# Attention in a two-layer decoder trunk: value products and divisions one query block behind the transposed probabilities

## The reference

```python
def causal_attention(q, k, v):
    ...
    def one_block(args):
        blk, qi = args
        sc = jnp.einsum("bqhd,bkhd->bhqk", qi, k).astype(jnp.float32)
        q_idx = blk * Q_BLOCK + jnp.arange(Q_BLOCK)
        sc = jnp.where(key_idx[None, :] <= q_idx[:, None], sc, neg)
        p = jax.nn.softmax(sc, axis=-1).astype(v.dtype)
        return jnp.einsum("bhqk,bkhd->bqhd", p, v)
```

## Time and profile before

| | before |
|---|---|
| median of 3 runs | 2352.89 us (2352.69 to 2354.26) |
| the profiled execution, its own time | 2351.72 us |
| its span | 2349.9 us |
| granted TensorE clock, mean over the span | 0.991 |
| busy: PE, DVE, ACT, POOL | 97%, 57%, 38%, 44% |
| attention stage, 205 to 425 us of the span | 220.0 us, PE busy 201.8 |

### The profile page before, as it was taken

One profiled execution on the slowest core, in us unless ns is written; L12 is line 12 of the kernel. 1 busy time (PEld: TensorE's weight loads), 2 busy tenths in 40 slices (PEclk: granted clock), 3 DMA queues, 4 the chain that ended last, 5 costly groups with the idle time before them and its releaser, 6 DMA issues.

```text
span 2349.9 us, 31829 instructions
## 1 busy us (share of the span) xinstructions
PE 2276.1 (97%) x10415; PEld 1850.8 (79%) x10415; DVE 1337.8 (57%) x2177; ACT 903.8 (38%) x1595; POOL 1034.3 (44%) x715
## 2 busy tenths in 40 slices
PE   6998999999999999999989999999999999999998
PEld 5786777778888888888868878878788888888886
DVE  7756565248755555555671115663875555555556
ACT  4535555124433333333441114451433333333333
POOL 3413333333555555555433332214335555555554
PEclk9999999999999999999999999999999999999998
DMA  4100000311111111111231110012111111111112
GB/s 167 45 27 1 1 0 28 117 36 45 37 54 53 47 52 46 52 54 54 64 124 55 45 45 28 27 56 92 34 36 54 54 53 47 52 46 52 54 54 90
DMA packets 34583, 122.07 MB, mean 52 GB/s; under 512 B 3840, under 2 KB 3968, under 8 KB 34240
## 3 DMA queue, kind: packets, MB, share of 16 engines
q1 hardware_dynamic: 31328, 105.39, 14.3%
q10 hardware_dynamic: 3168, 15.54, 1.7%
HBM read 112.52 MB, written 8.39 MB: 51 GB/s over the span
## 4 chain that ended last, share of the span: by engine, by line
PE 89%; DVE 7%; ACT 2%; issue 2%; POOL 0%; DMA 0%; ACTq 0%; DVEq 0%; POOLq 0%
PE ps L808 10%; PE ps L806 10%; PE ps L810 10%; PE ps L728 9%; PE ps L730 9%; PE ps L729 9%; PE ps L846 6%; PE ps L848 6%; PE ps L847 6%; PE ps L1571 2%; PE ps L1718 1%; PE ps L1722 1%; PE ps L1720 1%; PE ps L1559 1%; PE ps L603 1%
## 5 line engine op out<-in xcount | busy, mean ns | idle before, releaser
L509 POOL TENSOR_TENSOR wlo<-stage,whi 128x512 fp32r<-128x512 f32 x308 | 397.3, 1295 | 459.4 <-ACT whi L971 455.5
L728 PE MATMUL ps<-ahi,whi 128*128 128x512 f32 x896 | 368.8, 412 | 29.8 <-POOL wlo L434 19.1
L427 POOL TENSOR_TENSOR whi<-stage,cons 128x1024 fp32r<-128x1024 f32 x64 | 125.5, 1962 | 527.8 <-PE ps L730 313.4
L730 PE MATMUL ps<-ahi,wlo 128*128 128x512 f32 x896 | 351.2, 392 | 0.0
L729 PE MATMUL ps<-alo,whi 128*128 128x512 f32 x896 | 351.0, 392 | 0.0
L971 ACT CAST whi<-stage 128x512 fp32r<-128x512 f32 x308 | 189.2, 620 | 363.5 <-POOL stage L522 181.0
L1231 DVE TENSOR_TENSOR hT<-hT,ps 128x512 f32<-128x512 f32 x352 | 238.9, 686 | 153.9 <-PE ps L848 153.8
L846 PE MATMUL ps<-hid_hi,whi 128*128 128x512 f32 x640 | 251.3, 393 | 1.8 <-DVE hT L1231 1.6
L848 PE MATMUL ps<-hid_hi,wlo 128*128 128x512 f32 x640 | 249.8, 390 | 0.0
L847 PE MATMUL ps<-hid_lo,whi 128*128 128x512 f32 x640 | 249.6, 390 | 0.0
L806 PE MATMUL ps<-ahi,whi 128*128 128x512 f32 x608 | 236.7, 389 | 0.0
(11 more groups left out here) (323 smaller groups left out, 4089.6 us busy)
## 6 DMA issues: line engine op xcount, KB each, us to landing
stage<-in_wt SPq DMA_DIRECT2D x184, 512.0 KB, 3.6
hT<-in_xt SPq DMA_DIRECT2D x16, 256.0 KB, 9.6
hT<-in_xt ACTq DMA_DIRECT2D x8, 512.0 KB, 8.3
spill<-hT ACTq DMA_DIRECT2D x1, 4096.0 KB, 12.1
hT<-spill ACTq DMA_DIRECT2D x8, 512.0 KB, 8.2
out<-hT SPq DMA_DIRECT2D x16, 256.0 KB, 2.1
wqb_s<-in_wqb ACTq DMA_DIRECT2D x1, 1024.0 KB, 4.8
wlru_s<-in_wlru ACTq DMA_DIRECT2D x1, 512.0 KB, 6.4
```

What stands on the lines that cost most here:

```text
L509: nc.gpsimd.tensor_tensor(block_lo(c), src, block_hi(c).bitcast(F32), ALU.subtract).then_inc(sem(L + "b_ready"), 1)
L728: nc.tensor.matmul(bank, hi, rhs_k[0][:, tok], start=k_first, stop=False)
L730: return nc.tensor.matmul(bank, lo, rhs_k[0][:, tok], start=False, stop=k_last)
```

## The change

TensorE runs `weigh` for the step before, behind the transposes, scores and projection of the present step; the first step of a pair has none, and the last has two, its own behind that of step 14. VectorE does the same with `outputs`. The turns stay where they were, as do the queues of ScalarE, GpSimd and SyncE.

```diff
@@ TensorE, head_pair
                     if k < 4 and not (last and par == 1):
                         project(p * 2 + par + 1, 1 - par, k)
-                    weigh(p * 2 + par, k, step, grp)
+                    for before in ([i - 1] if i >= 1 else []) + ([i] if i == 15 else []):
+                        was, kb = before // 8, before % 8
+                        weigh(p * 2 + was, kb, p * 16 + before, p * 24 + (12 * was + groups_before[kb]))
                     for n, (slot, _, _) in enumerate(turns):
                         if par == 1 and slot == k:
                             turn(p, n, last)
@@ VectorE, head_pair
                     if k < 2 and not (last and par == 1):
                         rotate(p * 2 + par + 1, k)
-                    outputs(p, par, k, p * 16 + i)
+                    for before in ([i - 1] if i >= 1 else []) + ([i] if i == 15 else []):
+                        outputs(p, before // 8, before % 8, p * 16 + before)
                     for n, (slot, _, _) in enumerate(turns):
                         if par == 1 and k == min(slot + 1, 7):
                             y_lo(p, n)
```

## The result

| | before | with the change |
|---|---|---|
| median | 2352.85 us (2352.29 to 2354.26, 8 runs) | 2359.9 us (2357.89 to 2361.42, 8 runs) |
| ratio of the medians | | 1.0027, 95% interval 1.0018 to 1.0036 |
| profiled execution | 2351.72 us, span 2349.9 | 2359.52 us, span 2357.1 |
| granted TensorE clock, mean | 0.991 | 0.990 |
| second turn of pair 1, 2, 3, 4 starts at | 263.83, 318.14, 372.48, 423.63 | 266.20, 323.36, 379.88, 430.05 |

The changed kernel is slower by 0.27%, some 6.4 us by the ratio. Before: 54.31, 54.34, 51.15 us. With the change: 57.16, 56.52, 50.17.

The account below looks back on a forecast made before the run. TensorE, busy 97% of the span, was taken to bound the kernel. The profiled 2351.7 us plus 4.7 for the engines and 1.1 for the clock made 2357.5, with the median 1.2 higher at 2358.7; range 2350 to 2364.

Parts of the forecast that it names:

- term 1: First head's second projection: the moved value products no longer cover the scaling and rotation chain; cost 1.51 us per pair.
- term 2: Third projection of both heads: seven blocks of value products cover where eight stood; cost 0.22 us each, 0.44 per pair.
- term 3: Second head's second projection: four blocks cover instead of seven, and ScalarE is 0.45 us late; cost 1.02 us per pair.
- term 4: Value products' waits for copies of the transposed probabilities are removed; gain 1.88 us per pair.
- term 5: Step 5's transposes wait for the bank that step 4's first copy empties; cost 0.25 us per pair.
- term 6: Pair's end: step 15's value products wait for step 14's division, queued behind the next pair's maximum; cost 0.73 us per pair.
- term 7: Turn 1's wait and the first projection's 1.3 us wait for the pair's last turn both stay; later GpSimd splits cost nothing.
- last pair at full clock: Last pair: second head has no projections, so the lag has other work to run; the pair gives 1.5 us back.
- clock term: Pair ends: deeper gaps make three clock falls instead of one, 0.55 us each; +1.1 us.
- A: Waits ahead of value products go and nothing replaces them, saving 10.8 us; 2342.1 us, chance 0.08.
- B: About even: second-head and pair-end costs smaller, slow stretch at the stage's end shorter; 2349.8 to 2355.0 us, chance 0.27.
- C: The clock falls at every gap, +5.0 us instead of +1.1; 2362.6 us, chance 0.15.

Follow-up runs that it names:

- e12: The change plus six unread dummy matmuls in each gap, ahead of the first head's second projection and between the flushed value products; 2356.9 us, ratio 1.0013.
- e5: Kernel before, with the lag only in steps 0 to 3 of the first head in the loop's pairs, caught up in step 4; 2359.12 us, ratio 1.0024.
- e8: Kernel before, lag only from step 4 of heads, taken up before scores of steps 7 and 15, those divisions before the maximum; last head lagged throughout; 2346.42 us.
- e11: e8 with the first head's lag begun one step earlier, at step 3; 2346.75 us, ratio 0.997.
- e1: Kernel before, with the lag in the last pair alone; 2351.04 us, ratio 0.9985.
- e2: The change, with the last pair back in the old order, so the lag is in the loop alone; 2361.11 us, ratio 1.0033.
- e4: The change, with step 14's value products ahead of step 15's scores and their division ahead of the maximum, in the loop; 2356.27 us, ratio 1.001.
- e7: Kernel before, with only step 14's value products and division deferred to step 15 in the loop, the flush alone; 2359.45 us, ratio 1.0027.
- e6: The change, with step 0's value products back in step 0 and none in step 1, moving the gap behind the second projection; 2365.92 us, ratio 1.0058.
- e9: The change plus twelve unread dummy matmuls in each gap, ahead of the first head's second projection and between the flushed value products; 2362.21 us, ratio 1.0038.
- e10: e6 plus twelve unread dummy matmuls in each gap, ahead of the first head's third projection and at the pair's end; 2363.5 us, ratio 1.004.

## Why the prediction was right

The median came out 1.2 us above the forecast, and it is the case that was forecast, not another with the same sum. Term by term, with the full-clock pairs of e12:

| step | predicted | measured |
|---|---|---|
| P(0) to P(1), first head (term 1) | 4.46 us, a gap of 1.80 | 4.45, idle 1.61 (records overlap) |
| P(1) to P(2) (term 2) | 0.22 open | idle 0.22 and 0.24 |
| P(0) to P(1), second head (term 3) | 4.46 + 0.45 = 4.91 | 4.86 |
| copy waits (term 4) | all gone | no row left |
| T(5), first head (term 5) | 0.25 | 0.19 |
| end of the pair (term 6) | +0.73 | +0.84 |
| turns (term 7) | unchanged | 3.2 and 2.0, as before |
| loop pair at full clock | +2.07 | +2.2 (56.53 against 54.32) |
| last pair at full clock | -1.5 | -1.4 (48.28 against 49.7) |
| clock | +1.1 | +1.0 in the stage |

The 0.84 of term 6: from the last score's end (319.62, worked out from its start and 0.39 us) to W(15) are 2.12 us and from there to the turn 1.62, 3.74 in all, less W(14) with its 0.61; before, 0.66 and 1.63. The 49.7 is an estimate: e5 has the last pair of before, 50.22 us with one slow stretch, less the 0.55 that the prediction read for one. By the prices found below it may be off by 0.3.

The three loop pairs cost the engines 2.2 us each (the first, from P(0) to its turn, 53.93 against 51.74) and the last pair gives 1.4 back: 5.2 us, predicted 4.7. Another 0.2 stands ahead of the first P(0) (212.27 against 212.09), where nothing was moved. For the clock, the change is 2.5 us over e12 behind the first turn (0.6 in the second pair, 1.9 in the last), and before has 1.5 in its last pair (51.15 against the estimate of 49.7): 1.0 more, predicted 1.1. The three make the 6.4 us between 423.63 and 430.05. The slow stretch at the start of the stage is no part of this: it lasts to 212 both in before and in the change. In e12 it ends at 209, ahead of the first dummy, and its P(0) comes 0.8 us earlier for a reason that is not the filling.

Another 0.8 of the span's 7.2 lies behind the stage, where nothing was to move. One row of PE's waits there differs, first of before, then of the change:

```profile
PE ps L620 <- DVE diag L681: 4.5, 3, 2.2
```

```profile
PE ps L620 <- DVE diag L681: 6.3, 3, 3.8
```

The same row has 6.3 us in e8 and e12, and 4.4 and 4.3 in e5 and e11. It follows no part of the change; I take it for scatter between executions, which no run was made to show. In the traces of this case the part of the span behind the last turn took between 1925.0 us (e11) and 1931.2 (e1), with the same code.

In the last pair the new waits were as listed (W(7) 0.36 and W(11) 0.54 for 0.55 each, T(13) 0.32 for 0.3, W(15) 0.45 for 0.5), but for T(9) with 0.31, which was not foreseen, and W(14), which did not wait.

The signs that the prediction had named came too: PE's idle time ahead of the first projection matmul is 10.4 us (9.7 and 0.7), no product waits for a copy, W(15) waits 1.50 us, the loop pairs take over 56 and the last is shorter. Its limit of three slow stretches is met only if the one at the start of the stage, which it did not count in before either, is left out.

**What was off is the make-up of the clock term.** Its total came out by luck, since three things came otherwise than counted and offset each other. The count was too high: three falls at the loop's pair ends were forecast and two came. The price, "a fall costs 0.55, as the waits swallow the rest", holds for the short stretches: those of some 3.4 us cost 0.4 and 0.7 in two pairs of e2, 0.65 in e4 and in e5, 0.8 in e1 and 0.6 in the change. It fails for the one at the third pair's end, which lasted from 379.3 to 386.2, twice as long, and cost 1.9; P(1) came 5.70 us behind P(0) there (382.82 to 388.52), so no wait took it up. And the fall of before at 420.1, ahead of its last turn and worth 0.9 of the 1.5, was kept in the sum; in the change it came at 430.5, behind the last turn. So, with the estimate of 49.7, +0.6, +1.3 and -0.9 stand where two times 0.55 was forecast. In e7 and e6 no such offset helped, and the excess was 1.0 to 1.3 and 2.5 to 4.7 us a pair.

**The rivals.** A was wrong where it said it would be, at P(1) 4.45 us behind P(0); e1 shows the piece of it that is true, in the last pair. B needed terms 3 and 6 to be smaller; they were 0.97 (4.86 less 4.46, and the 0.57 of cover) and 0.84, for 1.02 and 0.73. C, the clock at every gap, didn't come for the change, whose second pair end stayed at 1.00; e6, with the gap one interval on, is nearly that case.

The Trainium skill, page TensorE: Matmul & The Clock Gate, section Loop structure matters more than you think, has matmuls stay at full clock when they run back to back, and lose it at a long wait for a DMA between them. e12 agrees with the first, at 1.00 until 427 with its gaps filled. The prediction carried the second over to short waits, of which the section says nothing: here the clock fell in a kernel with gaps of at most 1.61 us, and stayed up with them filled; the change's second pair end, with a gap of 1.50 us and a clock of 1.00, shows that not every one does.

**What stays open**: why the clock fell at some of the equal gaps and not at others, also between executions of the same code, so that the count of slow stretches in one trace is only a rough one; and why the gap ahead of P(2) brought more slow stretches than the one ahead of P(1). And e8 is 8.2 us ahead at the last turn (415.46 against 423.63) but 6.2 at the end of the span; the row on diag holds 1.8 of that.

## What to carry to other kernels

Before work is moved out of the way of a wait, ask what chain it covers where it stands: 1.5 us of value products under a projection's scaling and rotation were worth more than the copy waits that they suffered. A lag pays where the engine has other work and no chain runs beneath (e1, e8). Its flush is best spread ahead of the last scores (e4 gained half a microsecond a pair by it), with the short operation it waits for put ahead of the long one in the other queue; e8 has both, and no run shows the second alone. Where a change opens short gaps on TensorE, allow for the clock beside their length, and test that with dummy matmuls that just fit.

## What the runs showed of the hardware that was not expected

- With 84 more matmul records (10499 against 10415) that nothing reads, the changed kernel was 3 us faster (2356.9 against 2359.9 us, ratios 1.0013 and 1.0027), its granted clock at 1.00 from 209 to 427 us of the span and its mean clock 0.991 to 0.994 in eleven executions, against 0.988 to 0.991 in eight.
- Behind the start of the stage no gap that the trace shows ahead of a value product, a projection or a turn was longer than 1.61 us in the change and 1.75 in e6, and the clock fell to 0.50 in both. A slow stretch of the change cost 0.6 us where it lasted 3.3 us and waits took it up, and 1.9 where it lasted 6.9.
- A 128x128 matmul of two plain float32 operands, as the dummies are, is two records in the trace, and twelve such matmuls took 2.73 us, 0.23 each; a transpose of the same size is one record (eight blocks in T(1), x8). I had sized the fillers by half of that, which is why those of e9 and e10 overran.
